# Sliding attention in units of 128 queries and four heads, with the mix split for the out-projection by token chunks

## What is computed

```python
# chunks of 64 tokens; a query of chunk n sees the 16 meta keys and the keys of chunks n-1 and n
s_band = jnp.einsum('bnqhgd,bnkhd->bhgnqk', qc, kb)
key_shift = WINDOW_CHUNKS - 1 - jnp.arange(WINDOW_CHUNKS * CHUNK) // CHUNK
valid = jnp.arange(n)[:, None] >= key_shift[None, :]
s_band = jnp.where(valid[:, None, :], s_band, -jnp.inf)
s_meta = jnp.einsum('bnqhgd,bkhd->bhgnqk', qc, km)
p = _softmax_with_sink(jnp.concatenate([s_meta, s_band], axis=-1), sink)
o_r = einsum(p[..., :N_META], vm) + einsum(p[..., N_META:], vb)
...
mix = jnp.concatenate([sb_o, sw_o], axis=-1)
return h + jnp.einsum('ble,ed->bld', mix, w_out)
```

## Time and profile before

| | |
|---|---|
| median of 3 runs | 1393.2 us (1391.79 to 1398.45) |
| profiled execution | 1392.5 us |
| its span | 1390.7 us |
| mean granted TensorE clock | 0.955 of full |
| HBM read, written | 50.21 MB, 12.71 MB |

### The profile page before, as it was taken

How to read it: one execution, slowest core, us unless ns; L and a number is a source line. 1 busy time by engine, 2 the same in 40 slices (tenths; PEclk the granted TensorE clock), 3 DMA queues, 4 the chain that set the end, 5 groups by cost and what they waited for, 6 DMA issues and landing times.

```text
span 1390.7 us, 23502 instructions
## 1 busy us (share of the span) xinstructions
PE 1274.6 (92%) x9314; PEld 1162.3 (84%) x9314; DVE 819.4 (59%) x1560; ACT 450.9 (32%) x1239; POOL 235.3 (17%) x96
## 2 busy tenths in 40 slices
PE   4699999999898999979979999999989899997996
PEld 3598888988787888869969898888878788886995
DVE  5926555464766777652392664546475677765327
ACT  4313333233243333331131333333324333333113
POOL 1421111011010010232142111011101101023211
PEclk7699999999999999989999999999999999997998
DMA  4511110111001110031311111011100010103103
GB/s 160 192 46 31 31 32 16 31 31 32 16 17 23 25 24 24 31 123 47 138 61 46 31 31 29 19 31 31 27 21 16 16 31 16 32 31 120 50 16 121
DMA packets 96075, 64.24 MB, mean 46 GB/s; under 512 B 35920, under 2 KB 89424, under 8 KB 95968
## 3 DMA queue, kind: packets, MB, share of 16 engines
q1 hardware_dynamic: 94960, 61.22, 14.6%
q10 hardware_dynamic: 864, 1.35, 0.3%
q0 software_dynamic: 144, 0.18, 0.1%
HBM read 50.21 MB, written 12.71 MB: 45 GB/s over the span
## 4 chain that ended last, share of the span: by engine, by line
PE 75%; DVE 15%; issue 5%; ACT 3%; POOL 1%; DMA 0%; SPq 0%; DVEq 0%; ACTq 0%; POOLq 0%
PE psum L605 34%; PE psum L610 16%; PE psum L661 6%; PE psum L690 5%; PE psum L673 5%; DVE dvT L1172 3%; DVE mix L1068 2%; PE psum L726 2%; DVE X L1248 2%; PE psum L754 1%; PE psum L728 1%; PE psum L757 1%; DVE small L1245 1%; PE psum L722 1%; PE psum L739 1%
## 5 line engine op out<-in xcount | busy, mean ns | idle before, releaser
L605 PE MATMUL psum<-UH,WH 128*128 128x344 f32 (+1 forms) x1632 | 548.5, 336 | 21.2 <-DVE UL L1075 8.3
L605 PE MATMUL psum<-UL,WH 128*128 128x344 f32 (+1 forms) x1632 | 532.8, 327 | 0.0
L610 PE MATMUL psum<-UH,WL 128*128 128x344 f32 (+1 forms) x1616 | 523.9, 324 | 0.4 <-POOL WL L1358 0.4
L605 PEld LDWEIGHTS psum<-UH,WH 128*128 128x128 f32 x1632 | 314.9, 193 | 40.0 <-issue 15.6
L1358 POOL TENSOR_TENSOR WL<-w_raw,WH 128x1024 fp32r<-128x1024 f32 x68 | 174.2, 2563 | 1024.1 <-DVE WH L1116 1024.1
L605 PEld LDWEIGHTS psum<-UL,WH 128*128 128x128 f32 x1632 | 314.4, 193 | 0.4
L610 PEld LDWEIGHTS psum<-UH,WL 128*128 128x128 f32 x1616 | 309.4, 191 | 1.4 <-POOL WL L1358 1.4
L1193 DVE TENSOR_TENSOR_SCAN X<-X,stick 16x16 f32<-16x16 f32 (+5 forms) x144 | 123.9, 903 | 29.6 <-ACT X L956 29.4
L966 ACT ACTIVATE PT<-psum 128x512 f32<-128x512 f32 (+6 forms) x328 | 130.9, 440 | 22.3 <-PE psum L673 11.4
L956 ACT ACTIVATE X<-psum 128x264 f32<-128x264 f32 (+9 forms) x240 | 91.2, 432 | 82.8 <-PE psum L661 82.6
L1196 DVE TENSOR_TENSOR_SCAN X<-X 128x352 f32<-128x352 f32 (+4 forms) x96 | 94.7, 1027 | 29.5 <-ACT X L956 29.5
(11 more groups left out here) (129 smaller groups left out, 1498.1 us busy)
## 6 DMA issues: line engine op xcount, KB each, us to landing
w_raw<-in_w_in SPq DMA_DIRECT2D x36, 512.0 KB, 3.7
h_spill<-X SPq DMA_DIRECT2D x16, 520.0 KB, 5.1
X<-h_spill SPq DMA_DIRECT2D x16, 520.0 KB, 5.2
w_raw<-in_w_in SPq DMA_DIRECT2D x32, 256.0 KB, 3.7
w_raw<-in_w_out SPq DMA_DIRECT2D x16, 256.0 KB, 2.8
w_raw<-in_w_out SPq DMA_DIRECT2D x32, 128.0 KB, 3.3
out<-X SPq DMA_DIRECT2D x6, 512.0 KB, 4.2
mix<-in_x SPq DMA_DIRECT2D x3, 512.0 KB, 5.6
```

The lines of the kernel that those rows point to most:

```text
L605: pe.matmul(bank[:, 0:width], WH[:, j % 2, k, :], u[:, k, chunk_uses(c)], start=(k == 0 and u is UH), stop=False)
L610: ins = pe.matmul(bank[:, 0:width], WL[:, j % 2, k, :], UH[:, k, chunk_uses(c)], start=False, stop=(k == KT - 1))
```

## The change

- **Units.** `UNITS` lists 18 units a layer: two head groups hp (slots 2hp and 2hp + 1), each with eight pairs of 64-token chunks and one meta unit. A unit is 4 heads by 128 queries. Each 64-token chunk u has its own 144 keys (16 meta, 128 band), laid out in `SKH`/`SKL` so that they are one slice; the columns of `SQ` hold both slots of a chunk side by side. No mask is needed, `kv_pad`, `windowb` and `identb` are gone. A unit takes both score banks, one for each key head.
- **Scores** are fp32r products of high and low parts over 64 rows, 12 matmuls of 144 columns a unit.
- **Turns**: four transposes of 128 keys ("main") and two of 48 rows ("meta"); values: one matmul of 256 columns for meta and first-chunk keys of both heads, four of 128.
- **Rope**: the raw projection is copied to `dvT`, SyncE swaps the halves by four DMAs into `vT`, VectorE does two multiplies and an add one task later, ScalarE and GpSimd write high and low parts another task later.
- **Gates**: slots 0 and 1 are multiplied as values come out, slots 2 and 3 by chunk. **Split** of the mix is by token chunk and in three groups of rows: 0 to 3 (low part on GpSimd), 4 to 5 and 6 to 7 (on VectorE).
- **Order**: the last stick-breaking pair has four tiles as fill (sv, sk, sq0, sq1), the sliding part six. `EARLY_OUTS` is empty. `OUT_ORDER` is 4, 5, 6, 7, 2, 3, 0, 1. `WEIGHT` of Z is 1.0 instead of 1.5.
- **Chunks** are 400, 384, 256 columns.

```diff
-CHUNKS = [(0, 352), (352, 344), (696, 344)]
+CHUNKS = [(0, 400), (400, 384), (784, 256)]
...
+    def swa_fill():
+        tasks = proj("sv", 0) + proj("sk", 0) + proj("sq", 0) + proj("sq", 1)
+        tasks[3] += [("turn_sv", 0), ("turn_sv", 1), ("turn_sv", 2)]
+        tasks[4] += [("turn_sv", 3), ("turn_sv", 4)]
+        for kind, s in (("sg", 0), ("sg", 1), ("sq", 2), ("sq", 3), ("sg", 2), ("sg", 3)):
+            tasks += proj(kind, s)
+        return delayed(tasks)
...
+    def swa_attention(first, last):
+        out = []
+        for n in range(first, last):
+            out += [("ST", n, part) for part in (("main", "meta") if UNITS[n][1] != META_UNIT else ("meta",))]
+            if n + 2 < len(UNITS):
+                out.append(("SZ", n + 2))
+            out += lagged([], [("SAV", n)])
+            if n + 1 < len(UNITS):
+                out.append(("SD", n + 1))
...
+    steps += [("SZ", 0)] + window[12] + lagged([], []) + window[13] + [("SZ", 1), ("SD", 0)] + flat(window[14:18])
+    steps += merge(swa_attention(0, HALF), window[18:24], 0.3, 1.2)
+    late = merge(swa_attention(HALF, len(UNITS)), window[24:], 0.5, 1.5) + lagged([], [])
+    for n, (hp, r) in enumerate(UNITS):
+        c = unit_chunk(r)
+        if hp == 1 and n + 1 == units_until(1, c):
+            at = max(late.index(("SAV", n)), late.index(("proj", TILE_OF["sg", 3], c))) + 1
+            late[at:at] = [("gate", c), ("split", c, 2)]
+    for c in range(3):
+        at = late.index(("proj", TILE_OF["sg", 3], c)) + 1
+        late[at:at] = [("split", c, 0), ("split", c, 1)]
...
+                def swap(e, c):
+                    sp.wait_ge(raw_in.sem, raw_in.at(l, 3 * e + c + 1))
+                    if e == 0:
+                        sp.wait_ge(turned.sem, turned.at(l, TURN_AT["turn_sv", 4] + 1))
+                    for a in range(0, 128, HD // 2):
+                        other = a ^ (HD // 2)
+                        sp.dma_start(swapped_of(c)[a:a + HD // 2, :], raw_of(c)[other:other + HD // 2, :])\
+                            .then_inc(raw_swapped[c].sem, 16)
...
+                    if j == IN_TILES:
+                        pe.wait_ge(ml_made_g.sem, ml_made_g.at(l, split_count(c, 0, (0,))))
+                        pe.wait_ge(ml_made_v.sem, ml_made_v.at(l, split_count(c, 2, (1, 2))))
...
                 def window_scores(step):
+                    n_unit = step[1]
+                    (hp, r), use = UNITS[n_unit], Z_AT[step]
+                    pe.wait_ge(rope_low_made.sem, rope_low_made.at(l, 3 * (2 + 2 * hp) + unit_chunk(r) + 1))
+                    for g in range(2):
+                        pe.wait_ge(z_read.sem, z_read.at(l, use + g - Z_RING + 1))
+                    keys_h, keys_l = (t[:, :, :].rearrange("p r k -> p (r k)") for t in (SKH, SKL))
+                    for u in range(unit_columns(n_unit)[0]):
+                        first, count, at = keys_of(r, u)
+                        a, rows_out = (0, 32) if r == META_UNIT else (32 + 128 * (2 * r + u), 128)
+                        for i, (low, keys) in enumerate(((0, keys_h), (0, keys_l), (1, keys_h))):
+                            for g in range(2):
+                                rows = slice(64 * g, 64 * g + 64)
+                                q = SQ[rows, 2 * hp + low, a:a + rows_out]
+                                z = z_bank[0:rows_out, g, 144 * u + at:144 * u + at + count]
+                                ins = pe.matmul(z, q, keys[rows, first:first + count], start=(i == 0), stop=(i == 2))
...
+                def rope_add(step):
+                    _, e, c = step
+                    dve.wait_ge(raw_swapped[c].sem, raw_swapped[c].at(l, 64 * (e + 1)))
+                    dve.wait_ge(raw_in.sem, raw_in.at(l, 3 * e + c + 1))
+                    link(dve.tensor_tensor(swapped_of(c), swapped_of(c), sinT[:, chunk_uses(c)], ALU.mult))
+                    link(dve.tensor_tensor(raw_of(c), raw_of(c), cosT[:, chunk_uses(c)], ALU.mult))
+                    dve.tensor_tensor(raw_of(c), raw_of(c), swapped_of(c), ALU.add).then_inc(rope_added.sem, 1)
```

More of the change, by code:

```diff
@@ L109, in sb_unit, with delayed @@
         return v + q + k + g
[L111 to L131, removed]
+    def delayed(tasks):
+        out = [list(task) for task in tasks] + [[], []]
+        for i, task in enumerate(tasks):
+            for step in task:
+                if step[0] == "proj" and ORDER[step[1]][0] in ("sk", "sq"):
+                    e = rope_tile(*ORDER[step[1]][:2])
+                    out[i + 1].append(("rope_add", e, step[2]))
+                    out[i + 2] += [("rope_high", e, step[2]), ("rope_low", e, step[2])]
+        return out
+    def swa_fill():
[5 more added lines that the diff above has]
+        return delayed(tasks)
     def lagged(turn, value):
@@ L202, in layer_steps @@
         j = IN_TILES + i
[L203 removed]
+        steps += ([("proj", j, c)] if (i, c) not in EARLY_OUTS else []) + [("add", i, c), ("square", i, c)]
         waiting_sum.append(("sum", i, c))
@@ L957, in stick_scores, with copy_turned @@
                                        ACT.Sigmoid, scale=-SCALE).then_inc(z_read.sem, 1)
-                def copy_turned(step, key, parts):
-                    use, slot = TURN_AT[step], PT_AT[key]
+                def copy_turned(step, rows, width):
+                    use, slot = TURN_AT[step], PT_AT[step]
                     act.wait_ge(turned.sem, turned.at(l, use + 1))
@@ new lines, in window_scores @@
+                    use, nq, (units, w) = Z_AT[step], unit_rows(n_unit), unit_columns(n_unit)
+                    if n_unit >= P_RING:
+                        act.wait_ge(turned.sem, turned.at(l, LAST_TURN[PAIRS * BLOCKS + n_unit - P_RING] + 1))
+                    act.wait_ge(peaked.sem, peaked.at(l, n_unit + 1))
+                    low, diff, total = (unit_numbers(n_unit, i) for i in (1, 2, 3))
+                    act.activation(by_unit(diff, n_unit), by_unit(diff, n_unit), ACT.Exp).then_inc(sink_exp.sem, 1)
@@ L1235, in window_peak @@
-                    link(dve.scalar_tensor_tensor(out=m[:, 2:4], in0=m[:, 0:2], scalar=-SCALE, in1=sink,
+                    n_unit = step[1]
+                    use, nq, (units, w) = Z_AT[step], unit_rows(n_unit), unit_columns(n_unit)
+                    peak, low, diff = (by_unit(unit_numbers(n_unit, i), n_unit) for i in range(3))
+                    dve.wait_ge(z_full.sem, z_full.at(l, use + 2))
+                    scores = z_bank[0:nq, :, 0:units * w].rearrange("q g (u k) -> q g u k", u=units)
@@ new lines, in window_peak @@
+                    if UNITS[n_unit][1] == 0:
+                        dve.memset(window_weights(n_unit)[:, 0:4:2, 0:64], 0.0)
+                        dve.tensor_reduce(peak[:, :, 0], scores[:, :, 0, 64:], AX.X, ALU.max)
+                        link(dve.tensor_reduce(peak[:, :, 1], scores[:, :, 1, :], AX.X, ALU.max))
+                    else:
+                        link(dve.tensor_reduce(peak, scores, AX.X, ALU.max))
+                    link(dve.scalar_tensor_tensor(out=low, in0=peak, scalar=-SCALE, in1=unit_sink(n_unit),
```

640 lines of the change are left out of this document (331 added, 309 removed).

## The result

The changed kernel takes **1471.4 us** (median of 4 runs, 1471.16 to 1473.0), the kernel before 1393.2 in the same comparison: a ratio of 1.0554 (95% interval 1.052 to 1.0588). The forecast was 1320, with 1288 to 1356 as its range. It was wrong in size and in sign.

A forecast was written before the change was run, and what follows sets the result against it. TensorE, busy 92% of the span, was taken as the bound. A layer: matmuls -30.3, idle -2.7, tail -3.1, sum -36.1 us; twice, -72.2 from 1392.5 gives 1320 us, range 1288 to 1356.

The forecast's parts named there:

- Part 1: Attention matmuls on TensorE in the sliding stretch: a new unit takes 2.6 us, saving 1.9; 30.3 us saved a layer.
- Part 2: Rope ahead of the sliding stretch: swaps take 4.7 us, all but one hidden; TensorE idle 4 us instead of 10.8.
- Rival (b): Swaps on SyncE's queue stand in one row, VectorE waits 3.7 us in 30 passes: +111, 1431 us; chance 0.06.
- Part 3: Order in the sliding stretch: rounds of 4.8 us, nothing lost beside a projection chunk; idle 9 us instead of 4.9.
- TensorE idle in rounds that have a projection: Sliding stretch: listed among the signs that would show the forecast wrong; no size given.
- Part 4: Tail after the last projections: 29 us, between 24 and 36, against 32.1 that count before; saving 3.1 a layer.
- Rival (c): Tail: the early start doesn't come, gates and splits lengthen it to 37 us, eight more a layer, 1336; chance 0.14.
- Part 5: Chunks of 400, 384, 256 for 352, 344, 344: taken as 0, between -3 and +4 us a layer.
- Rival (a): GpSimd locks VectorE in each round, 4.8 + 2.0 = 6.8 us: 17 us a layer, 1354; chance 0.13.

The follow-up runs named there:

- experiment 3: The changed kernel with the weighing of the next unit listed ahead of the maxima of the one after it and of the value step: 1365.29 us, ratio 0.9799.
- 7: Two kernels, the changed one with VectorE's list alone altered: values' copy behind the next weighing, 1444.16 us; weighing right behind the maxima, 1378.96 us.
- 4: The changed kernel with the last six projection chunks spread over more rounds of the second half (pace 1.0 for 1.5): 1481.39 us, ratio 1.0629.
- Experiment 2: The changed kernel with two unused 512-column matmuls ahead of TensorE's wait for the weighing in each unit: 1447.69 us, ratio 1.0387.
- experiment 1: The kernel before with only the chunk sizes changed to 400, 384 and 256: 1387.41 us, ratio 0.9958.
- experiment 6: The kernel of experiment 3 with VectorE's split rows (4 and 5) listed ahead of GpSimd's (0 to 3): 1365.01 us, ratio 0.9805.

## Why the prediction was wrong

**Part 1, matmul arithmetic: right.** A unit takes 2.69 us at full clock, forecast 2.6; its scores 0.82, forecast 0.87. So a unit saves 1.8 us of the 1.9, and the 30.3 us a layer hold to within 5% where the clock is full. Projection matmuls of 256 columns start 0.12 apart, forecast 0.121.

**Part 2, rope: nearly right.** The swaps landed in 2.0 us (median of the 50 KB ones), taken 1.9 from 64 KB. The stretch from 360 has 5.75 us idle, forecast 4, before 10.8. One swap was exposed, as said, but by more: 7.8 us on VectorE, forecast 4.7. The page's row of the swaps (count, size, median us to landing):

```profile
vT<-dvT SPq DMA_DIRECT2D x40, 50.0 KB, 2.0
```

VectorE's waits for them, from 340 to 650:

```profile
DVE vT L1289 <- DMA vT<-dvT: 9.1, 2, 7.8
```

Rival (b), the slower one, named this queue. It is refuted: 9.1 us of waits over the first layer's rope, not 55.

**Part 3, the order: here it failed.** The step is the sentence "Where a projection chunk (24 x 0.159 = 3.8) stands in the round, TensorE has 2.6 + 3.8 = 6.4 and nothing is lost." It compared lengths: the round's chain through the engines, 4.8 us, is shorter than 6.4. It did not ask where in VectorE's list the weighing stands relative to that chunk. In the diff the weighing comes last in each round, behind the maxima of unit n + 2 and behind the value copy, and `merge` puts the chunk among these. An engine that takes its steps in order gives the overlap only if the step that TensorE needs stands ahead of the step that needs TensorE. Experiments 3, 7 and 4 show it three ways: moved ahead of everything, 106 us come back; moved ahead of projection parts, gates and copy alone, 92; with chunks spread over more rounds, the waits stay at 59.7 us a layer and 10 us are lost. The prediction named the sign of it ("TensorE idle in rounds that have a projection"), and it had walked SyncE's queue step by step, but not VectorE's.

**The clock: a term that wasn't in the sum.** The earlier trace rows has the sign of it: the tail of the kernel before, with 12.4 us idle of 35.5, ran at 0.76. The forecast doubled nothing in the sliding stretch when idle time came in, since by its sum there was hardly any. With 37.1 us idle the clock was 0.79 and 101.75 us of work became 129.05. The Trainium skill, "TensorE: Matmul & The Clock Gate", "HAM oscillation — how this bites in real kernels", tells of a kernel whose groups of matmuls are split by waits and which therefore starts each next group at the low clock. This trace agrees: projection matmuls of 400 columns in this stretch start 0.33 apart up to 545.41 and 0.18 apart from 545.59 on, within one chunk, which follows two units whose transposes had waited 1.8 us each. Idle time is thus paid more than once: 37.1 us as such and 27 in the work around it, 1.7 times in all. Experiment 2 shows that the clock has a part of its own: idle time was filled with work that nothing uses and 24 us came back.

**Part 4, the tail: the round was right, the rest not.** A round without a chunk was to be 4.8 us. At full clock it would be 2.69 + 1.8 = 4.5. At half clock it is 6.82. The tail has 50.3 us against 29; with the order mended it has 36.1, at a granted clock of 0.57, which is the upper end of the forecast's own 24 to 36. The value of 29 took TensorE's share at full clock. Rival (c) had the right kind (the tail gets longer) at 37 us, which is what the mended order has, and less than half of the changed kernel's excess.

**Part 5, the chunks: the number right, by luck.** 0, between -3 and +4 a layer, was forecast; experiment 1 has -5.3 for the program, so -2.7 a layer. But the forecast put any gain at the boundary, by the shorter chain of chunk 2, and none in the projections. The boundary got 1.6 us longer, as the longer chain of chunk 0 would have it, and the stretches with projections beside attention got 1.3 to 2.3 us shorter each.

**Rival (a)**, GpSimd locking VectorE, is seen in single rows: the split above, 3.69 for 0.99; and in rope, 2.58 us for a full-width multiply of 384 columns beside GpSimd's 2.58, forecast 0.57:

```profile
519.82 2.58 DVE L1290 TENSOR_TENSOR dvT<-dvT,cosT 128x384 f32<-128x384 f32 x1
```

The Trainium skill, "SBUF — State Buffer", "Who interferes with whom", says such pairs exclude each other for the length of an instruction, and the durations agree, also that of the four-column add in experiment 6. The rival is neither refuted nor priced: experiment 6 moved the lock from the splits to the weighing, and no run took it away, in the splits or in rope. It isn't the cause of the miss, since experiment 3 gives 106 us back with the same operations on GpSimd; but it may be in what remains.

**What remains of the miss** once the order is mended is 1365.3 against 1320. The stretch and tail of experiment 3 have 162.9 us against the 139.8 forecast, 23 a layer, 46 in all: 16.0 in the stretch and 7.1 in the tail. Of the 16.0, idle time is 2.8 (11.8 for 9), and TensorE's busy time is 13.3 (115.03 for 101.75), at a clock of 0.87. The waits in the stretch are 4.7 us for the low part of the queries' rope on GpSimd (the other of the two ends where the stretch begins) and 4.7 for the weighing. In the tail it is 7.9 for the weighing, in two waits, and both follow rows that the lock stretches: VectorE's splits and the weighing's first multiply take 3.75, 3.67, 2.42 and 2.18 us between 551 and 571, where their forms take 0.99, 0.96, 0.69 and 0.23 beside an idle GpSimd. That is 9.1 us of VectorE's time, so by this estimate the lock alone could account for the tail's two waits. How the tail's 7.1 divide between lock, clock, gates and splits wasn't tried apart.

## What to carry to other kernels

When several engines walk one list, price a move by the position of each engine's part and not by the sum of its durations: for every step that the bounding engine waits for, write down what stands ahead of it on its own engine, and ask of each whether it waits for the bounding engine. Here moving a 1.3 us step past such neighbours was worth 106 us of 1471, with the same instructions. Price an idle gap of TensorE at more than its length where the clock row already shows that gaps lower it, and look for a place ahead of dense work, not amid it, if idle time is to be filled on purpose.

## What the runs showed of the hardware that was not expected

- **Unused matmuls can pay.** 70.8 us of them made the changed kernel 24 us faster, and 25.3 us of them in the tail made the mended one 7 us faster; 1.3 us a layer of that is the out-projection behind, which began at full clock. In a stretch that TensorE bounds they cost 10 and 23 us.
- **Waits cost more than their length.** 37.1 us of idle time in the sliding stretch came with some 27 us of extra busy time for the same work (clock 0.79). In the tail a round's 2.69 us of matmuls took 5.0.
- **A lock between VectorE and GpSimd moves when its victims are reordered.** VectorE's splits went from 3.75 and 3.67 us to 0.99 and 2.29, and the four-column add behind them from 0.15 to 3.40, until GpSimd was done; the time went from 1365.29 to 1365.01.
